# Sums of squares in two attention layers: the squares as a high and a low part of the one-pass float32 form

## What is computed

```python
def l2_norm(x):
    return x * lax.rsqrt(jnp.sum(x * x, axis=-1, keepdims=True) + NORM_EPS)

def gated_deltanet(xn, w_in, conv_w, a_log, dt_bias, o_norm, w_out):
    ...
    q = l2_norm(qkv[..., :DN_QK].reshape(b, s, DN_HEADS, DN_DK).astype(jnp.float32)) * (DN_DK ** -0.5)
    k = l2_norm(qkv[..., DN_QK:2 * DN_QK].reshape(b, s, DN_HEADS, DN_DK).astype(jnp.float32))
    ...
    o = chunk_gated_delta_rule(q, k, v, beta, g_log)
    o = rms_norm(o, o_norm) * jax.nn.silu(z.reshape(b, s, DN_HEADS, DN_DV).astype(jnp.float32))
    return o.reshape(b, s, DN_V).astype(xn.dtype) @ w_out

def shared_dilated_kv(h, kv_norm, w_kv, k_norm):
    ...
        k = rms_norm(kv[:, :, g, 0], k_norm[g])

def dilated_attention(xn, w_q, q_norm, w_out, kv_blocks):
    ...
        qg = rms_norm(q[:, :, g], q_norm[g])
```

## Time and profile before

| | before |
|---|---|
| median of 3 runs | 1817.9 us (1817.21 to 1818.48) |
| the profiled execution | 1808.5 us |
| its span, first to last instruction | 1806.7 us |
| TensorE busy | 1719.9 us, 95% |
| VectorE, ScalarE, GpSimd busy | 683.8, 443.2, 114.1 us |
| queries and keys of layer 1, from 58.0 to 182.9 us | TensorE busy 122.43 of 124.90 us |
| recurrences and output of layer 1, to 400 us | TensorE busy 216.23 of 217.10 us |
| experts of layer 1, to 960 us | TensorE busy 531.42 of 560.00 us, transfers 381 GB/s |
| key heads, 960.0 to 1035.2 us | TensorE busy 68.80 of 75.20 us |
| values and query heads, to 1196 us | TensorE busy 157.32 of 160.80 us |
| experts of layer 2, from 1250 us | TensorE busy 523.54 of 556.70 us, transfers 363 GB/s |

### The profile page before, as it was taken

How to read it: one execution, slowest core, us unless ns; L and a number is a source line. 1 busy time by engine, 2 the same in 40 slices (tenths; PEclk the granted TensorE clock), 3 DMA queues, 4 the chain that set the end, 5 groups by cost and what they waited for, 6 DMA issues and landing times. The chain is left out here.

```text
span 1806.7 us, 19800 instructions
## 1 busy us (share of the span) xinstructions
PE 1719.9 (95%) x7340; PEld 829.7 (46%) x7340; DVE 683.8 (38%) x1342; ACT 443.2 (25%) x666; POOL 114.1 (6%) x174
## 2 busy tenths in 40 slices
PE   7999999997999999998998999998899999989898
PEld 4555566643334434333355565564343443433343
DVE  5666444414234334232332113356233433423241
ACT  5555133312011011010124606543101101101020
POOL 0034700000000000000000000000000000000000
PEclk9999999998999999999999999999999999999999
DMA  8122232275999999999971020036899999999941
GB/s 277 50 80 67 84 82 71 82 291 215 408 420 420 420 420 420 421 421 421 413 266 47 1 102 0 1 140 248 348 421 420 421 420 420 421 421 422 421 180 47
DMA packets 109577, 481.06 MB, mean 266 GB/s; under 512 B 22208, under 2 KB 39360, under 8 KB 58304
## 3 DMA queue, kind: packets, MB, share of 16 engines
q1 hardware_dynamic: 104896, 471.64, 65.1%
q0 software_dynamic: 4608, 8.40, 1.3%
HBM read 476.33 MB, written 12.06 MB: 270 GB/s over the span
## 5 line engine op out<-in xcount | busy, mean ns | idle before, releaser
L1905 PE MATMUL bank<-ring,xT 128*64 128x512 f32 x2048 | 463.5, 598 | 30.4 <-DMA ring<-in_w 30.0
L1905 PEld LDWEIGHTS bank<-ring,xT 128*64 128x64 f32 x2048 | 142.5, 137 | 295.7 <-issue 274.9
L1857 DVE TENSOR_TENSOR H<-H,bank 128x512 f32<-128x512 f32 x240 | 154.0, 683 | 311.6 <-PE bank L1893 311.6
L1929 PE MATMUL bank<-ring,sg 128*64 128x512 f32 x1024 | 228.3, 598 | 0.0
L1929 PEld LDWEIGHTS bank<-ring,sg 128*64 128x64 f32 x1024 | 70.7, 137 | 134.2 <-issue 126.2
L639 PE MATMUL bank<-ring,ring 128*128 128x512 f32 x256 | 127.5, 607 | 0.0
L624 PE MATMUL bank<-ring,ring 128*128 128x512 f32 x256 | 112.9, 593 | 0.0
L2273 PE MATMUL bank<-ring,ring 128*128 128x512 f32 x256 | 110.5, 592 | 0.0
L1847 DVE SCALAR_TENSOR_TENSOR low<-bank,weight_now,high 128x512 fp32r<-128x512 f32 x64 | 48.0, 751 | 159.0 <-ACT high L1951 155.7
L1945 ACT ACTIVATE sg<-bank 128x512 f32<-128x512 f32 x32 | 19.1, 597 | 360.7 <-PE bank L1914 360.7
L1893 PE MATMUL bank<-high,Sb 128*128 128x512 f32 x240 | 106.8, 445 | 0.0
(11 more groups left out here) (326 smaller groups left out, 1930.7 us busy)
## 6 DMA issues: line engine op xcount, KB each, us to landing
ring<-in_w SPq DMA_DIRECT2D x192, 2048.0 KB, 31.4
ring<-in_w_heads SPq DMA_DIRECT2D x16, 1024.0 KB, 5.2
ring<-in_w_ple_gate SPq DMA_DIRECT2D x4, 2048.0 KB, 28.7
ring<-in_w_kv SPq DMA_DIRECT2D x3, 2048.0 KB, 21.4
ring<-in_b_w_q SPq DMA_DIRECT2D x3, 2048.0 KB, 20.8
inverses<-ring SPq DMA_DIRECT2D x16, 256.0 KB, 4.0
ring<-in_a_w_out SPq DMA_DIRECT2D x2, 2048.0 KB, 8.0
ring<-inverses SPq DMA_DIRECT2D x16, 256.0 KB, 3.1
```

The lines of the kernel that those rows point to most:

```text
L1857: dve.tensor_tensor(out, out, k.bank[6 + j % 2][:, :], ALU.add).then_inc(s.added, 1)
L1905: last = pe.matmul(out[e * SLOTS:(e + 1) * SLOTS, :], k.xT[:, at, e * SLOTS:(e + 1) * SLOTS], w[:, e, c, :], start=(at == 0), stop=(at == ...
L1929: last = pe.matmul(k.bank[2 + n][e * SLOTS:(e + 1) * SLOTS, :], k.hT[:, c, e * SLOTS:(e + 1) * SLOTS], w[:, e, c % 2, n * HALF:(n + 1) * H ...
```

## The change

The square of a head is made twice by ScalarE: once into an fp32r tile (`sq_high`, rounded to the one-pass form) and once in float32 as before. A subtraction makes the rest, also as fp32r (`sq_low`). TensorE then adds up both with one-pass matmuls into the same bank, with ones of type fp32r (`ones_r`). The subtraction is on VectorE in layer 1 and on GpSimd in layer 2. On VectorE the low parts of queries and keys stand at the head of `keys(h)`, ahead of the next convolution, and that of the outputs in `tokens(h)` between the masks and the scaled keys. In layer 2 the query heads' sum moves from behind the second to behind the fourth matmul of the next projection (`c == 3` for `c == 1`). Semaphores `low` and `olow` take the place of `sq` and `osq` in TensorE's waits.

```diff
+def sum_of_squares(pe, k, out, n):
+
+    pe.matmul(out[:, :], k.ones_r[:, :], k.sq_high[:, n, :], start=True, stop=False)
+    return pe.matmul(out[:, :], k.ones_r[:, :], k.sq_low[:, n, :], start=False, stop=True)
+
+
+def low_square(eng, k, square, n):
+
+    return eng.tensor_tensor(k.sq_low[:, n, :], square, k.sq_high[:, n, :], ALU.subtract)
...
     act.wait_ge(g.early, k.n_early)
+    act.activation(k.ones_r[:, :], k.ones, ACT.Copy).then_inc(g.cb, 1)
...
                 for j in range(2):
-                    pe.wait_ge(s.sq, 2 * h + j + 1)
-                    pe.matmul(bank[(2, 7)[j]][:, :], k.ones, k.sqr[:, j, :], start=True, stop=True).then_inc(s.ssq, 1)
+                    if h == 0 and j == 0:
+                        pe.wait_ge(g.cb, 1)
+                    pe.wait_ge(s.low, 2 * h + j + 1)
+                    sum_of_squares(pe, k, bank[(2, 7)[j]], j).then_inc(s.ssq, 1)
...
-                pe.wait_ge(s.osq, h + 1)
+                pe.wait_ge(s.olow, h + 1)
                 wait(pe, s.ln_o, h)
-                pe.matmul(bank[2][:, :], k.ones, k.osq[:, :], start=True, stop=True).then_inc(s.oss, 1)
+                sum_of_squares(pe, k, bank[2], 0).then_inc(s.oss, 1)
...
                 vbase = 3 * h
+                for j in range(2):
+                    dve.wait_ge(s.sq, 2 * h + j + 1)
+                    low_square(dve, k, k.sqr[:, j, :], j).then_inc(s.low, 1)
                 if h + 1 < HEADS:
                     conv_qk(h + 1, 0)
...
+            def low_output(h):
+
+                dve.wait_ge(s.osq, h + 1)
+                low_square(dve, k, k.osq[:, :], 0).then_inc(s.olow, 1)
...
+                if h:
+                    low_output(h - 1)
                 dve.wait_ge(s.kt, h + 1)
...
+            low_output(HEADS - 1)
             outputs(HEADS - 1)
...
                     act.wait_ge(s.sil, 2 * h + j + 1)
+                    act.activation(k.sq_high[:, j, :], k.qk[:, h % 2, j, :], ACT.Square)
                     act.activation(k.sqr[:, j, :], k.qk[:, h % 2, j, :], ACT.Square).then_inc(s.sq, 1)
...
+                act.activation(k.sq_high[:, 0, :], bank[7][:, :], ACT.Square)
                 act.activation(k.osq[:, :], bank[7][:, :], ACT.Square).then_inc(s.osq, 1)
...
+    act.activation(k.sq_high[:, n % 2, :], bank[:, :], ACT.Square)
     act.activation(k.sqr[:, n % 2, :], bank[:, :], ACT.Square).then_inc(s.sq, 1)
+
+
+def low_head(pool, k, s, n):
+
+    pool.wait_ge(s.sq, n + 1)
+    low_square(pool, k, k.sqr[:, n % 2, :], n % 2).then_inc(s.low, 1)
...
-            pe.wait_ge(s.sq, j + 1)
+            pe.wait_ge(s.low, j + 1)
             if j >= 2:
                 pe.wait_ge(s.ln, j - 1)
-            pe.matmul(bank[4 + j % 2][:, :], k.ones, k.sqr[:, j % 2, :], start=True, stop=True).then_inc(s.sums, 1)
+            sum_of_squares(pe, k, bank[4 + j % 2], j % 2).then_inc(s.sums, 1)
...
-                pe.wait_ge(q.sq, n + 1)
+                pe.wait_ge(q.low, n + 1)
                 wait(pe, q.ln, n)
-                pe.matmul(bank[SUMS][:, :], k.ones, k.sqr[:, n % 2, :], start=True, stop=True).then_inc(q.sums, 1)
+                sum_of_squares(pe, k, bank[SUMS], n % 2).then_inc(q.sums, 1)
...
-                    if n and c == 1:
+                    if n and c == 3:
                         sums(n - 1)
...
+        @block.gpsimd
+        def _(pool):
+            for n in range(keys.heads):
+                low_head(pool, k, kv, n)
+            for n in range(LAST):
+                low_head(pool, k, q, n)
...
+        k.ones_r = sb("ones_r", [P, P], F32R)
...
+            k.sq_high, k.sq_low = (sb(name, [P, 2, SEQ], F32R) for name in ("sq_high", "sq_low"))
```

More of the change, by code:

```diff
@@ L548, in delta_semaphores @@
      s.exported, s.blocks, s.init, s.inv, s.flipped, s.returned, s.C, s.tok, s.v_turned, s.X, s.Xs, s.Y, s.Vs,
-     s.Z, s.Ts, s.W, s.nW, s.u, s.us, s.dS, s.St, s.o, s.osq, s.oss, s.ln_o, s.rn_o, s.og_step, s.og) = (
+     s.Z, s.Ts, s.W, s.nW, s.u, s.us, s.dS, s.St, s.o, s.osq, s.oss, s.ln_o, s.rn_o, s.og_step, s.og, s.low, s.olow) = (
          k.sem(f"dn_{name}") for name in
@@ L554, in delta_semaphores @@
              "X", "Xs", "Y", "Vs", "Z", "Ts", "W", "nW", "u", "us", "dS", "St", "o", "osq", "oss", "ln_o",
-             "rn_o", "og_step", "og"))
+             "rn_o", "og_step", "og", "low", "olow"))
     s.qk_landed = [k.sem(f"dn_qk_landed{i}") for i in range(2)]
@@ L1113, in feature_semaphores @@
     s = norm_semaphores(k, tag)
-    (s.proj, s.sq, s.sums, s.ln, s.rn, s.out, s.scaled, s.vproj, s.v, s.xh, s.xh_odd, s.xq) = (
+    (s.proj, s.sq, s.sums, s.ln, s.rn, s.out, s.scaled, s.vproj, s.v, s.xh, s.xh_odd, s.xq, s.low) = (
         k.sem(f"{tag}_{name}") for name in
-        ("proj", "sq", "sums", "ln", "rn", "out", "scaled", "vproj", "v", "xh", "xh_odd", "xq"))
+        ("proj", "sq", "sums", "ln", "rn", "out", "scaled", "vproj", "v", "xh", "xh_odd", "xq", "low"))
     return s
```

## The result

| | before | after |
|---|---|---|
| median of four runs each | 1817.56 us | 1805.04 us |
| lowest and highest | 1815.09, 1818.48 | 1803.57, 1806.17 |
| the profiled execution, its span | 1808.5, 1806.7 | 1806.17, 1804.4 |
| TensorE busy | 1719.9 us | 1710.2 us |
| VectorE, ScalarE, GpSimd busy | 683.8, 443.2, 114.1 us | 702.3, 464.9, 140.8 us |

The ratio of after to before is 0.993, with a 95% interval of 0.9918 to 0.9943: 12.7 us faster, between 10.4 and 14.9. The forecast was 11.4 us less, a median of 1806.5. But the two profiled executions differ by 2.3 us only. The trace of before came from an execution 9 us under its own median, and the experiments have to say why before its time is split up.

A forecast was written before the change was run, and what follows sets the result against it. TensorE, busy 1719.9 of 1806.7 us, was taken as the bound. The terms -5.1 - 3.2 + 0.6 - 3.7 = -11.4 us took the median from 1817.9 to 1806.5, range 1801.5 to 1815.5.

The forecast's parts named there:

- The pair: Two one-pass matmuls replacing a four-pass sum on TensorE: 0.46 us instead of 0.86, a gain of 0.40 when alone.
- (b): Rival: the switch to one-pass exposes the weight load, a lone pair costs 0.67 us; -5.1 us, 1812.8; chance 0.10.
- (c): Rival: the switch costs the whole gain, a lone pair takes 0.86 us; -0.7 us, 1817.2; chance 0.13.
- (f): Rival: the change does not do what it says, the form runs in more than one pass; chance 0.01.
- Stage A: Query and key sums of the first layer, 8 heads: -5.1 us, from -5.5 + 0.1 + 0.3.
- Stage B: The 8 output sums in the first layer's recurrences: 8 x 0.40 gained, -3.2 us.
- Stage C: Sums of 6 key heads, second layer: -4 x 0.40 + 1.6 + 0.6 = +0.6 us, a loss.
- Stage D: Sums of 12 query heads, second layer: -11 x 0.40, plus 0.7 wait before the first scores, -3.7 us.
- (d): Rival: GpSimd's subtraction takes about 3 us, query sums 1 to 3 wait 0.8 each; -5.6 us, 1812.3; chance 0.07.
- (e): Rival: GpSimd's subtraction takes 5 us or more, 11 query sums wait; 1823 us, slower; chance 0.07.
- first call: GpSimd's first low part in the second layer's key sums: some 6 us by the skill, 5 us more loss, sum near -6.
- The clock: TensorE's fall to 1.2 GHz from 184.00 to 190.60 may not recur or another may come: 3.3 us on both sides.

The follow-up runs named there:

- the second trace of before: The kernel before, unchanged, timed and profiled once more: 1815.66 us, ratio 0.9998.
- stage A alone: The changed kernel with four-pass sums put back for layer 1's outputs and all of layer 2, pairs only for layer 1's queries and keys: 1812.05 us, ratio 0.9972.
- the whole: The changed kernel, unchanged, measured and profiled again on the chip of its halves: 1803.48 us, ratio 0.9931.
- layer 2 alone: The changed kernel with four-pass sums put back in the first layer, pairs only in the second: 1814.34 us, ratio 0.9982.
- the experiment with the earlier place: The changed kernel with layer 2's query sums put back behind the second matmul of the next projection: 1808.09 us, ratio 0.9951.
- the slowest kernel: The changed kernel with every pair issued twice: 1823.96 us, ratio 1.0036.

## Why the prediction was right, and where not

The sum of the stages is 11.8 us where 11.4 was forecast: A, B and D came within 0.1 each, and C was 0.6 off.

**The pair** was the term with the widest bounds, and it came out at the value taken: 0.46, with no edge and no exposed weight load at equal tile shape. Rivals (b), (c) and (f) fall with it. Behind a wait the first step of a pair is 0.34 instead of 0.23 (990.48 to 990.82). At seven of the eight output sums it is 0.31 or 0.32 without a wait, behind the products of 128x64 (228.27 to 228.58 in after). The four-pass sum took 0.91 there instead of 0.86 (234.80 to 235.71 in before), so such a sum gains 0.36, a little less than the 0.40 of the forecast.

**Stage A** was 5.1 and is 5.1 at the products of head 7. From head to head, heads 1 to 4 and 7 gain 0.79 each and two heads, while GpSimd inverts, 0.74 and 0.60: a loss of 0.24 where 0.3 was put. Head 0 waits 0.20 and 0.24 and loses some 0.2 instead of 0.1 (what a wait costs beyond its record stands below). "The gain passes" into the recurrence held, but not for the reason given. The prediction looked at VectorE's L861 alone; before, TensorE waits 2.48 for it and then for L875. TensorE's waits from 181 to 207 us in the second trace of before:

```profile
PE bank L713 <- DVE ring L861: 2.5, 1, 2.5
PE bank L722 <- DVE ring L875: 0.7, 1, 0.7
```

In after the transfer of the inverses is what comes last, with one wait of 3.63 in place of the two. In the trace with stage A alone 1.3 of the 5.1 us gained are gone as the recurrence begins (180.06 against 183.85): the sign "earlier by 5" didn't come, it is 3.8. At the first W all is back and 0.5 more. 0.7 is the second wait that is gone. Most of the rest, 1.1, is the place of a fall of the clock. It is 6.83 us long in both, but before it lies on work, and in the other trace its first 1.78 us lie in the wait for the transfer, where the lower level costs nothing; half of that is 0.9. The second trace of before, then the one with stage A alone:

```profile
185.12:191.95 6.83, 6.79 (x20) 4.59 (x20) 3.23 (x6) 0.00 (x0) 1.33 (x5) 0.50 0.57 199
```

```profile
178.28:180.06 1.78, 0.00 (x0) 0.00 (x1) 1.68 (x4) 0.00 (x0) 0.00 (x0) 0.50 1.00 276
```

Stage A was forecast right on TensorE's own queue. That all of it was kept into the recurrence is in part luck: the transfer took 1.3, and the lost second wait and the place of the fall gave it back. What a larger gain would have met at that transfer isn't shown.

**Stage B**: 3.2 forecast, 3.1 measured in the whole.

**Stage C**: a loss of 0.6 forecast, 0.0 measured. The step that failed is the first key sum, with 1.6 put and 0.6 measured by the marks of the kernel with layer 2 alone. Two things were wrong. 0.55 were put for a first operation of GpSimd, which took 1.26 like all others, and the wait is 0.74 instead of 1.5. The row of 0.82 for 36 elements was read as a cost of idleness, but its own idle time is 0.2 us, as a MEMSET runs just ahead of it. GpSimd's first operation after a long rest stood in the trace of before and took 0.36:

```profile
117.06 0.36 POOL L574 TENSOR_TENSOR ring<-Lb,Tb 64x31 f32<-64x31 f32 x1 [105.17 <-DMA Lb<-L_blocks]
```

And the sum took the wait in full without the 0.40 that this pair saves like any other; by the prediction's own 1.5 the loss is 1.1. The last key sum loses 1.0, not 0.6: it waits 2.05, and the value projections then 0.48 instead of 1.35; the prediction counted only the added square of the chain through ScalarE and not that TensorE now stands still ahead of it, with the sum itself later. The two errors of the stage, 1.0 and 0.4, partly cancel.

**A wait costs more than its record.** The first key sum, with layer 2 alone: 0.75 less 0.40 is 0.35, and the marks say 0.63. With the query sums at their old place, each wait of 0.83 moves the next mark by 1.11. With GpSimd's work doubled, waits of 0.31 to 0.33 move it by 0.60. That is 0.28 beyond the record each time, of which 0.11 is the longer first step; no run shows what the rest is. The prediction had no such term. It also closes stage D: 11 x 0.40 less 0.52 and 0.28 is 3.6.

**Stage D**: 3.7 forecast, 3.6 and 3.5 measured. The wait before the first scores is 0.52 where 0.7 was put, and the sums one to three have none; the experiment with the earlier place shows what these would have cost. The last query sum waits 0.58, which the list of signs doesn't have, but it stands ahead of the long wait and costs nothing. Rivals (d) and (e) fall with GpSimd's 1.28 us. The "first call" of 6 us, which the prediction drew from the Trainium skill (GPSIMD Engine Reference, section 2.1), didn't come: the first low part took 1.26. But GpSimd had run the same kind of operation 128 times by then, the first at 9.68 us, so this was no first call, and no run here tests the page. The rule of section 4.1 of the same page of the Trainium skill, GpSimd at about half of VectorE's rate, agrees: 1.28 against 0.685.

**The clock** was left at zero with 3.3 on both sides. What the prediction did not see is that the base itself had it: 1808.5 was an execution with 7 us less lost to the lower level than the second one. It was right to carry the sum to the median as a difference, and right to count no cost of the clock: in the timed executions its mean is the same before and after. A reader who had set the two profiled executions against each other would have called the change a gain of 2 us. One fall may come with the change. Behind the wait of 2.05 for the last key sum the clock falls in both traces of after, and not in the kernel with layer 2 alone, which has the same wait; the stretch from 1020 to 1040 of each:

```profile
1020.00:1040.00 20.00, 17.95 (x73) 14.89 (x72) 3.88 (x6) 13.75 (x18) 1.26 (x1) 0.91 0.00 0
```

```profile
1020.00:1040.00 20.00, 17.48 (x67) 12.24 (x66) 4.14 (x6) 17.03 (x22) 2.01 (x2) 1.00 0.00 0
```

Of the six traces whose last key sum waits 1.6 us or more, four have a fall there, of the six others none. Such a fall lasts 3.41 us and costs half of that, 1.7 us. Whether the wait brings it stays open. So does the fall near 970 (985 in the slowest kernel): all nine traces of kernels with pairs in the first layer have it, 6.8 us long in eight of them, and of the three others only the second of before, for 3.4.

## What to carry to other kernels

A float32 sum over partitions by a matrix of ones costs 0.86 us here and, as a pair of one-pass matmuls, 0.46, and the price is a second square and a subtraction on engines with slack: place these in gaps that the timeline shows, and keep the four-pass form (the old one) where the sum follows its square at once. Before an operation is pulled ahead, look for what stands before its consumer in that engine's queue: a sum whose root waits for an exponential gains nothing. Set profiled executions against each other only after a look at the granted clock of each, and count their times from the same instruction ahead of the change; a sum of terms read from one trace is carried to the median as a difference.

## What the runs showed of the hardware that was not expected

- A change from a four-pass to a one-pass float32 matmul and back costs nothing at equal tile shape: steps of 0.23 us, and 0.79 us gained per head of two sums. Behind products of 128x64 the first step is 0.31 or 0.32.
- A wait of TensorE ahead of a pair costs 0.28 us beyond its recorded length, for waits of 0.31, 0.74 and 0.83 alike.
- GpSimd's subtraction of 128x512 takes 1.26 to 1.30 us in all 18 instances, the first one after 151 us of idleness among them.
- Two traces of one kernel differ by 8.0 us of span, some 7 of them by the falls of the clock (mean granted clock 0.991 and 0.987). A fall that lies in a wait of TensorE costs nothing for as long as the wait lasts.
